# Moving SBUF operands by 32 bytes: three kinds of matmul operand at new offsets against the weights

## The reference

```python
# first_block
n = modulate(rmsnorm(h, g_ffn1), sh1, sc1); h = h + 0.5*gt1*swiglu(n, w1_gate, w1_up, w1_down)
n = modulate(rmsnorm(h, g_mix),  sh2, sc2); h = h + gt2*hybrid_mixer(n, w_in, w_pool, pool_scale, w_out)
n = modulate(rmsnorm(h, g_ffn2), sh3, sc3); h = h + 0.5*gt3*swiglu(n, w2_gate, w2_up, w2_down)
h = rmsnorm(h, g_final)
# second_block: two attention layers (sliding window with sinks; then causal blocks)
hn = rmsnorm_2(h, norm_g[i]); q, k, v, z = split_proj(hn, w_in)
o = attention(rope(q), rope(k), v) * silu(z); h = h + o @ w_out[i]
return rmsnorm_2(h, final_g)
```

## Time and profile before

| | before |
|---|---|
| median of 3 runs | 836.94 us (832.35 to 839.76) |
| the profiled execution | 835.18 us |
| its span, first to last instruction | 833.0 us |
| TensorE busy | 745.0 us (89%), mean granted clock 0.952 |
| VectorE, ScalarE, GpSimd busy | 545.7, 366.7, 121.2 us |
| read from HBM | 150.97 MB |

### The profile page before, as it was taken

One profiled execution on the slowest core, in us unless ns is written; L12 is line 12 of the kernel. 1 busy time (PEld: TensorE's weight loads), 2 busy tenths in 40 slices (PEclk: granted clock), 3 DMA queues, 4 the chain that ended last, 5 costly groups with the idle time before them and its releaser, 6 DMA issues.

```text
span 833.0 us, 14911 instructions
## 1 busy us (share of the span) xinstructions
PE 745.0 (89%) x6112; PEld 695.8 (84%) x6112; DVE 545.7 (66%) x782; ACT 366.7 (44%) x558; POOL 121.2 (15%) x77
## 2 busy tenths in 40 slices
PE   5699999999978976889999999994999977999984
PEld 4489999999957966779999999993887767888884
DVE  3589968877756345567478556557588756678741
ACT  3253433434325344435443343354465564665532
POOL 0051113223333521240004000002000000000000
PEclk9799999999978998898999999998899999999998
DMA  9986898777648882354568565552133324433201
GB/s 311 349 265 229 278 362 285 230 243 265 219 161 279 281 263 68 101 165 141 201 212 256 188 196 163 195 188 90 58 119 103 105 99 152 152 103 106 97 2 50
DMA packets 132455, 152.64 MB, mean 183 GB/s; under 512 B 2616, under 2 KB 126268, under 8 KB 132284
## 3 DMA queue, kind: packets, MB, share of 16 engines
q1 hardware_dynamic: 132324, 152.01, 56.3%
q10 hardware_dynamic: 88, 0.02, 0.0%
HBM read 150.97 MB, written 1.05 MB: 182 GB/s over the span
## 4 chain that ended last, share of the span: by engine, by line
PE 37%; DVE 8%; ACT 7%; issue 3%; POOL 0%; DVEq 0%; ACTq 0%; POOLq 0%
PE sc L1206 5%; PE sc L1208 5%; PE acc L1206 5%; PE sc L1207 5%; PE acc L1208 5%; PE acc L1207 5%; ACT prob L658 3%; DVE wlo L831 2%; ACT whi L568 2%; PE stat L1217 1%; PE acc L1432 1%; PE acc L1434 1%; PE acc L1433 1%; DVE rstd L851 1%; ACT probT L665 1%
## 5 line engine op out<-in xcount | busy, mean ns | idle before, releaser
L831 DVE TENSOR_TENSOR wlo<-raw,whi 128x2048 fp32r<-128x2048 f32 x105 | 259.2, 2472 | 133.4 <-ACT whi L568 133.2
L568 ACT ACTIVATE whi<-raw 128x2048 fp32r<-128x2048 f32 x105 | 200.2, 1907 | 76.0 <-PE sc L1208 63.4
L1206 PE MATMUL sc<-nhi,whi 128*128 128x256 f32 x704 | 200.7, 285 | 6.0 <-DVE nlo L870 4.1
L1207 PE MATMUL sc<-nlo,whi 128*128 128x256 f32 x704 | 199.4, 283 | 0.0
L1208 PE MATMUL sc<-nhi,wlo 128*128 128x256 f32 x704 | 199.3, 283 | 0.0
L1206 PEld LDWEIGHTS sc<-nhi,whi 128*128 128x128 f32 x704 | 134.7, 191 | 7.4 <-issue 4.5
L1207 PEld LDWEIGHTS sc<-nlo,whi 128*128 128x128 f32 x704 | 136.2, 193 | 0.0
L1208 PEld LDWEIGHTS sc<-nhi,wlo 128*128 128x128 f32 x704 | 135.1, 192 | 0.0
L1206 PE MATMUL acc<-nhi,whi 128*128 128x256 f32 x376 | 113.8, 303 | 18.2 <-DVE nlo L870 10.7
L1207 PE MATMUL acc<-nlo,whi 128*128 128x256 f32 x376 | 108.3, 288 | 0.0
L1208 PE MATMUL acc<-nhi,wlo 128*128 128x256 f32 x376 | 108.1, 287 | 0.0
(11 more groups left out here) (184 smaller groups left out, 1149.7 us busy)
## 6 DMA issues: line engine op xcount, KB each, us to landing
ada<-in_w_ada_dram SPq DMA_DIRECT2D x28, 1024.0 KB, 5.2
raw<-in_w_gate_dram SPq DMA_DIRECT2D x22, 1024.0 KB, 5.8
raw<-in_w_up_dram SPq DMA_DIRECT2D x22, 1024.0 KB, 5.5
raw<-in_w_down_dram SPq DMA_DIRECT2D x22, 1024.0 KB, 4.8
raw<-in_w_out_dram SPq DMA_DIRECT2D x12, 1024.0 KB, 5.3
raw<-in_w_in_b_dram SPq DMA_DIRECT2D x10, 1024.0 KB, 5.1
raw<-in_w_in_a_dram SPq DMA_DIRECT2D x9, 1024.0 KB, 5.2
raw<-in_w_in_dram SPq DMA_DIRECT2D x8, 1024.0 KB, 7.6
```

The lines of the kernel that those rows point to most:

```text
L568: nc.scalar.activation(whi[:, u % NS], raw[:, u % NS], ACT.Copy).then_inc(hi_done, 1)
L831: nc.vector.tensor_tensor(wlo[:, u % NS], raw[:, u % NS], whi[:, u % NS].bitcast(F32), ALU.subtract).then_inc(lo_done, 1)
L1206: mm(to, stat_hi, mov_hi, start=first, stop=False, skip_group_check=True)
L1207: mm(to, stat_hi, mov_lo, start=False, stop=False, skip_group_check=True)
```

## The change

Five small tensors (32 bytes of each partition each) are allocated at other places in the list. `junk` now lies ahead of `nhi`, `mx` and `nm` ahead of `hhi`, `den` and `esink` ahead of `yhi`. What follows each moves up by their sizes.

```diff
--- before.py
+++ after.py
@@ -203,6 +203,7 @@
         hT = sb("hT", [P, DC, S])
         tmp = sb("tmp", [P, 4, S + 8])
         pw = sb("pw", [P, 2, S + 8])
+        junk = sb("junk", [P, 8])
         nhi = sb("nhi", [P, DC, S], F32R)
         nlo = sb("nlo", [P, DC, S], F32R)
         sq = sb("sq", [P, 4, S])
@@ -210,6 +211,8 @@
         std = sb("std", [P, S])
         rstd = sb("rstd", [P, S])
         xo = sb("xo", [P, 2, D])
+        mx = sb("mx", [P, 4, 2])
+        nm = sb("nm", [P, 4, 2])
         hhi = sb("hhi", [P, 2, S], F32R)
         hlo = sb("hlo", [P, 2, S], F32R)
         kraw = sb("kraw", [P, 2, S])
@@ -222,6 +225,8 @@
         probT = sb("probT", [P, 2, SW])
         alibi = sb("alibi", [P, 2, SW])
         og = sb("og", [P, 2, S])
+        den = sb("den", [P, 4, 2])
+        esink = sb("esink", [P, 4, 2])
         yhi = sb("yhi", [P, DC, S], F32R)
         ylo = sb("ylo", [P, DC, S], F32R)
         consts = sb("consts", [P, C_END])
@@ -236,11 +241,6 @@
         sinks = sb("sinks", [P, 16])
         fgain = sb("fgain", [P, D])
         tiny = sb("tiny", [P, 4])
-        junk = sb("junk", [P, 8])
-        mx = sb("mx", [P, 4, 2])
-        nm = sb("nm", [P, 4, 2])
-        den = sb("den", [P, 4, 2])
-        esink = sb("esink", [P, 4, 2])
         rden = sb("rden", [P, 4, 2])
         fss = sb("fss", [P, 2, 4])
         fst = sb("fst", [P, 3, 2])
```

## The result

The changed kernel takes **840.92 us** (median of 18 runs, 835.7 to 843.2) against 836.2 (18 runs, 830.03 to 841.17): a ratio of **1.0051 (95% interval 1.0031 to 1.0072)**. That lies inside the range of 818 to 846, but on the other side of the forecast of 825: the kernel became slower by half a per cent, and the interval does not reach 1. The profiled execution took 840.93 us, its span is 839.1, 6.1 us longer than before. Clock and time of the changed kernel's runs go together: seven runs of 835.7 to 837.1 us have a mean granted clock of 0.958 to 0.961, eleven of 839.9 to 843.2 have 0.945 to 0.953. The profiled one is of the latter. The clock isn't all of the loss: of the runs of the kernel before that were timed beside the experiments, the seven with a clock of 0.957 to 0.963 took 828.3 to 834.9 us, mean 832.7, against 836.4 for the seven of the changed kernel.

What follows compares the result with a forecast made beforehand. TensorE's matmul spacing bounds the kernel; losing the higher level saves 6.4 (first feed-forward), 4.7 (second) and 2.2 us (mixers), 13.3 off 835.18: 821.9, 823.6 as median, plus 1.3 for stretches staying high: 825 us, range 818 to 846.

Steps and rivals of the forecast that it cites:

- What bounds the kernel: TensorE, busy 745.0 of 833.0 us; in the feed-forwards time is the number of matmuls times their spacing.
- The two levels and the break as a switch: Equal wide matmuls start 113.3 or 117.8 ns apart; a restart after a break can switch between them.
- a phase drawn anew has more to win there than to lose: New offsets likely end the higher spacing: 4.44 ns on 3235 wide matmuls against 4.44 ns on 1515.
- The bound from below: The weight load alone asks for 111 ns or so per wide matmul, so at most 25 us can be gained.
- Two streams of one engine that meet in the same memory: TensorE's weights and moving operand meet at a fixed phase, adding 6.8 ns at the higher level.
- No row shows a third level, so I price one more step of the same size: Upper bound on a new offset's price: 4.44 ns more per wide matmul.
- The other operands at nothing: Moved operands of VectorE, ScalarE, GpSimd and the DMAs were priced at no time.
- Rival A: Address beside the point, restarts alone set levels: 830 to 840 us, middle 836; within the no-change chance of 0.37.
- all wide matmuls' phase changes at once: A 32-byte shift moves where the operand streams meet by 8 floats, in every wide matmul.
- Rival B: Odd multiples of 32 bytes cost one more fetch per wide matmul: 850 or 856 us; slower by a step, 0.20.
- milder form: All 1515 wide matmuls at the lower level go up: +6.7 us, 843, counted as no change.
- Rival C: Kinds answer differently: nhi's gain alone 828.5 us (within the 0.43 for faster), hhi's alone 833 (within 0.37).

Runs made afterwards that it cites:

- all_zero: Kernel before with a 64-byte pad ahead of nhi, so nhi, hhi and yhi stand 0 bytes (modulo 256) off the weights: 844.62 us, ratio 1.0109.
- break_map: TensorE-only program, no model: units at 192 and 64 bytes behind breaks of 1 to 12 one-column matmuls; 113.3 or 117.8 ns per matmul.
- offset_map: TensorE-only program, no model: moving operand at 33 offsets, 0 to 1024 bytes off the weights; 113.3 to 120.0 ns per matmul, repeating every 256 bytes.
- cross_map: TensorE-only program that also moves the weights' start (0 to 192 bytes); equal starts give 120.0 ns, a difference of 96 gives 119.9.
- stream_modes: TensorE-only program with both operands streaming, or one held on one element: moving held 111.7 ns, weights held 113.3 at most offsets.
- nhi_alone: Kernel before with only nhi and nlo moved, to 224 bytes off the weights, hhi back at 192: 841.59 us, ratio 1.0068.
- longer_breaks: Kernel before, same addresses, with one-column matmuls added to the feed-forwards' breaks: 839.44 us, ratio 1.0036.
- nhi_hhi_112: Kernel before with nhi and hhi operands at 112 bytes off the weights (modulo 256), yhi left at 192: 827.69 us, ratio 0.9904.
- same_again: Kernel before, unchanged, run and profiled once more: 838.29 us (one run).
- hhi_yhi_alone: Kernel before with hhi moved to 32 and yhi to 96 bytes off the weights, nhi left at 192: 835.4 us, ratio 1.0013.
- all_112: Kernel before with nhi, hhi and yhi operands all 112 bytes off the weights (modulo 256): 829.52 us, ratio 0.9925.
- same_mod_128: Kernel before with 128-byte pads ahead of nhi, hhi and yhi, putting them at 64, 192 and 64 modulo 256: 837.37 us, ratio 1.002.

## Why the prediction was wrong, step by step

**What bounds the kernel: right.** The loss shows where the prediction put TensorE's spacing on the path. The second feed-forward pays what the spacing says: 2.4 us after, 6.0 in all_zero.

**The two levels and the break as a switch: right, read incompletely.** break_map confirms that a restart switches the level. The prediction kept "addresses alone don't set it" and then treated the address as a redraw of the same lottery. It is the address that decides which levels are in the lottery; the break, and what ran ahead of it, draws among them.

**The step that failed** is "a phase drawn anew has more to win there than to lose". It took the new offsets for a fresh draw between 113.3 and 117.8. offset_map has one price for each, 118.3, 116.7 and 120.0, and 113.3 for none of them; the kernel adds a rare 117.8 for hhi. Of the eight positions on the grid of 32 bytes, 64 and 192 are the only ones with the lower level; the kernel before had a mean of 116.4 ns with them, and the best of the other six is 32 with 116.7. The rows ahead of the prediction could not show that, as no row had another offset; but that was a reason to leave both signs alike, not to forecast 13.3 us of gain. What the levels did is worked out from the table, as an estimate: nhi 3040 intervals x 2.0 ns = 6.1 us, yhi 420 x 4.9 = 2.1, hhi near nothing, 8.2 us together; of that 2.4 show in the second feed-forward and 0.7 in the pool mixer, and the window mixer covers most of its own. The rest of the 6.1 us of span is chiefly the window mixer's 3.4, which go with the longer half-clock stretch, a term that the prediction didn't have. That this stretch stands in the profiled execution is in part luck: seven of the eighteen runs have the higher mean clock.

**The bound from below: right as a bound.** Nothing measured is under 111.7 ns, the spacing with the moving operand held, against 111 estimated from 128-column matmuls. That it is the load alone that asks for it is not shown, since that run still has 256 columns in each matmul.

**"Two streams of one engine that meet in the same memory": right** that it is two streams of one engine, by offset_map, cross_map and stream_modes; the place where they meet stays argued. The Trainium skill, "SBUF — State Buffer", "Who interferes with whom", gives TensorE independent ports for the two and no waiting. Here the rule doesn't hold: 120.0 ns against 111.7 for matmuls of the same size, nothing else running.

**"No row shows a third level, so I price one more step of the same size": wrong in size.** The steps are uneven, 113.3, 116.7, 117.8, 118.3, 120.0, and off this grid up to 123.

**The other operands at nothing: right**; VectorE's 1.9 us more lie in an engine that waits 134 us for `whi`.

**The rivals.** Rival A's 830 to 840 was missed by 1 us, and its mechanism is not what happened: the levels would have been mixed again, 399 and 385, and were 384 and 384. The sentence that all wide matmuls' phase changes at once was right. Rival B had the sign, at too great a size: 856 asked for 4.44 ns more on all, a mean of 120.8; all_zero, at 120.0, gives 844.6. Its milder form, "all 1515 go up, +6.7 us, 843", comes nearest to the run, though it put this down to the lower level's end and not to three offsets with three prices. Rival C, that the kinds answer differently, was right in form and wrong in sign.

**Open.** Whether a run has the longer half-clock stretch near 675 us. after (10.2 us of it) and nhi_alone (10.2) have it, longer_breaks and nhi_hhi_112 have 6.8 us in two pieces, before, same_again, hhi_yhi_alone and all_112 the short one of 3.4, same_mod_128 and all_zero none, each by one profile. That the window mixer's length follows it is seen: 120.9 and 121.4 us without it, 121.4 to 122.5 with 3.4, 123.0 and 123.1 with 6.8, 124.0 and 124.8 with 10.2. What picks it is not, and slower matmuls alone don't, by all_zero. Not settled either: whether 32 really holds two levels, and which level follows a break in the model kernel, where breaks are waits and not a number of matmuls.

## What to carry to other kernels

Where back-to-back matmuls reload their weights each time, count starts in a window of constant work and known clock before trusting mean durations: 285 ns stayed 285 ns while the spacing went from 113.3 to 118.3. For such matmuls the offset of the moving operand against the weights, modulo 256 bytes, is a parameter worth a map of its own in a small program: here two programs of 0.7 and 0.9 ms made it; it gave a 1% gain (112 bytes) and explained a loss (224, 96). When the trace holds one value of a parameter, a change of it has no sign yet; spacing at both of its levels is no evidence about a third value.

## What the hardware showed that was not expected

- The period of 256 bytes, and 112 bytes as a single good place between 120.0 and 121.8 ns, four bytes off on either side.
- One offset can hold two stable spacings, 113.3 and 117.8 ns, chosen by the number of one-column matmuls ahead and by what ran before them.
- Where the clock falls can weigh as much as the spacing: in the profile after, 6.8 us more at the half clock go with 3.4 us of loss in the window mixer, the slower matmuls with 2.4 in the second feed-forward. With every matmul at 120.0 ns (all_zero) TensorE stood at the half clock for 12.8 us less than before, and the loss came out 4 us and more below the expected; how much of that the clock gave back was not taken apart.
